# Spreading the relative-bias rows from SBUF in one transfer instead of by way of DRAM in two

## What is computed

```python
def run_trunk(x, ...):
    h = rmsnorm(x, g_attn)
    qa, ka, va, qb, kb, vb = split(h @ w_in)
    oa = window_sink_attention(qa, ka, va, sink_a, rel_bias)
    ob = axial_qknorm_attention(qb, kb, vb, gq_b, gk_b)
    x = x + concat(rmsnorm(oa), rmsnorm(ob)) @ w_out
    x = x + expert_choice_moe(rmsnorm(x, g_ffn), ...)
    x = x + sigmoid(rmsnorm(x, g_ple) @ w_ple_gate) * (p @ w_ple_proj)
    return rmsnorm(x, g_final)

# in window_sink_attention: 128 queries by 384 keys, 8 heads
rel = kj - WINDOW - qi
bias = rel_bias[t5_bucket(rel)]        # (128, 384) per head
s = q @ k * scale + bias
```

## Time and profile before

| | |
|---|---|
| Median of 3 runs | 1531.67 us (1531.56 to 1531.7) |
| The profiled execution | 1531.56 us; its span, first to last instruction, 1529.8 us |
| TensorE (PE) busy | 1422.8 us, 93% of the span |
| VectorE, ScalarE, GpSimd busy | 905.6, 728.1, 193.1 us |
| Mean granted TensorE clock | 0.964 |
| ACT's DMA queue, q10 | 1056 packets, 2.11 MB, 0.4% of 16 engines' span |
| Projection stage | about 0 to 243 us, TensorE busy 229.15 us of it |

### The profile page before, as it was taken

One profiled execution on the slowest core, in us unless ns is written; L12 is line 12 of the kernel. 1 busy time (PEld: TensorE's weight loads), 2 busy tenths in 40 slices (PEclk: granted clock), 3 DMA queues, 4 the chain that ended last, 5 costly groups with the idle time before them and its releaser, 6 DMA issues. The chain is left out here.

```text
span 1529.8 us, 21337 instructions
## 1 busy us (share of the span) xinstructions
PE 1422.8 (93%) x7224; PEld 1003.9 (66%) x7224; DVE 905.6 (59%) x1316; ACT 728.1 (48%) x1161; POOL 193.1 (13%) x257
## 2 busy tenths in 40 slices
PE   7999998999999788799999699999999999959997
PEld 5888886655555455588877456666666666638885
DVE  4644446777777588323377656766776676662433
ACT  5544446776667577322224444445444444433342
POOL 1211110000000000100001201211121122011220
PEclk9999998999999799899999799999999999989998
DMA  9444446122112324444334647787788778772331
GB/s 350 153 145 144 144 175 222 66 103 94 67 58 93 126 84 149 139 158 155 122 122 173 226 185 260 248 264 257 260 272 263 254 258 270 253 222 109 124 138 69
DMA packets 83750, 266.78 MB, mean 174 GB/s; under 512 B 8128, under 2 KB 37952, under 8 KB 68336
## 3 DMA queue, kind: packets, MB, share of 16 engines
q1 hardware_dynamic: 75472, 238.80, 43.4%
q0 software_dynamic: 7168, 25.17, 7.1%
q10 hardware_dynamic: 1056, 2.11, 0.4%
HBM read 201.55 MB, written 66.60 MB: 175 GB/s over the span
## 5 line engine op out<-in xcount | busy, mean ns | idle before, releaser
L1922 DVE TENSOR_TENSOR moe_w_lo<-ring,moe_w_hi 128x2048 fp32r<-128x2048 f32 x96 | 220.4, 2296 | 157.8 <-ACT moe_w_hi L1858 157.8
L1858 ACT ACTIVATE moe_w_hi<-ring 128x2048 fp32r<-128x2048 f32 x96 | 184.0, 1918 | 198.4 <-PE moe_p_g L2044 122.2
L1566 PE MATMUL mix_p_big<-kept_out_w,mix_m_hi 128*128 128x512 f32 x384 | 126.0, 410 | 4.9 <-DVE mix_m_lo L1441 2.7
L555 PE MATMUL proj_p_out<-proj_w_hi,proj_h_hi 128*128 128x512 f32 x288 | 118.2, 410 | 10.4 <-DVE proj_w_lo L465 10.2
L2052 PE MATMUL moe_p_gu<-ring,moe_xT_r 128*64 128x512 f32 x512 | 116.9, 598 | 0.0
L555 PE MATMUL proj_p_out<-proj_w_hi,proj_h_lo 128*128 128x512 f32 x288 | 113.7, 395 | 0.0
L555 PE MATMUL proj_p_out<-proj_w_lo,proj_h_hi 128*128 128x512 f32 x288 | 113.5, 394 | 0.0
L1090 DVE TENSOR_REDUCE sample_ntop<-sample_p_s 128x1 f32<-128x1024 f32 x64 | 78.2, 1222 | 37.1 <-PE sample_p_s L913 36.4
L927 PEld LDWEIGHTS sample_p_t<-kept_ident_r,sample_probs_r 128*128 128x128 f32 x688 | 72.8, 141 | 23.3 <-ACT sample_probs L1028 6.7
L1566 PEld LDWEIGHTS mix_p_big<-kept_out_w,mix_m_hi 128*128 128x128 f32 x384 | 72.5, 194 | 21.6 <-DVE mix_m_lo L1441 2.9
L927 PE MATMUL sample_p_t<-kept_ident_r,sample_probs_r 128*128 128x128 f32 x688 | 79.9, 245 | 5.0 <-ACT sample_probs L1028 2.6
(11 more groups left out here) (291 smaller groups left out, 3087.3 us busy)
## 6 DMA issues: line engine op xcount, KB each, us to landing
ring<-in_w_gate SPq DMA_DIRECT2D x32, 1024.0 KB, 5.2
ring<-in_w_up SPq DMA_DIRECT2D x32, 1024.0 KB, 7.1
ring<-in_w_down SPq DMA_DIRECT2D x32, 1024.0 KB, 6.8
qT_d<-proj_qT SPq DMA_DIRECT2D x12, 1024.0 KB, 3.8
proj_xT<-in_xT SPq DMA_DIRECT2D x12, 512.0 KB, 4.2
proj_w_raw<-in_w_in SPq DMA_DIRECT2D x8, 768.0 KB, 7.0
proj_x<-in_x SPq DMA_DIRECT2D x12, 512.0 KB, 4.7
kT_d<-proj_kT SPq DMA_DIRECT2D x12, 512.0 KB, 3.5
```

What stands on the lines that cost most here:

```text
L555: mm = pe.matmul(p_out[:, s, cols], h[:, s, k, :], w[:, k, cols], start=(k == 0 and n == 0), stop=(k == KC - 1 and n == 2))
L1566: mm = pe.matmul(p_out[:, cols], m[:, s, k, :], ww[:, k, cols], start=(k == 0 and n == 0), stop=(k == KC - 1 and n == 2))
L1858: act.activation(w_hi[:, at % SPLIT], raw[:, at % RAW], ACT.Copy).then_inc(hi_made, 1)
L1922: dve.tensor_tensor(w_lo[:, at % SPLIT], raw[:, at % RAW], w_hi[:, at % SPLIT].bitcast(F32), ALU.subtract).then_inc(lo_made, 1)
```

## The change

The first of the two transfers, its semaphore `out` and the scratch tensor `rel_rows_d` are removed. One transfer remains, issued on ACT where the first one was, in front of the two squares. Its source is now the SBUF tile `rows`, on 8 partitions, each row named 128 times; its destination is as before, but the heads are now the outermost dimension of the access pattern (8), the query positions the second (128), where before the query positions were outermost. It still sets `stored`.

```diff
-        self.landed, self.looked, self.added, self.out, self.stored = (
-            a.sem(n) for n in ("bias_landed", "bias_looked", "bias_added", "bias_out", "bias_stored"))
+        self.landed, self.looked, self.added, self.stored = (
+            a.sem(n) for n in ("bias_landed", "bias_looked", "bias_added", "bias_stored"))
...
-    def store(self, act, rows_d):
+    def store(self, act, rel_d):
+
         act.wait_ge(self.added, 1)
-        act.dma_start(rows_d, self.rows[:]).then_inc(self.out, 16)
-
-    def spread(self, act, rows_d, rel_d):
-
-        act.wait_ge(self.out, 16)
-        act.dma_start(bass.AP(rel_d.tensor, 0, [[HEADS * (REL + P) + 1, P], [REL + P, HEADS], [1, REL]]),
-                      bass.AP(rows_d.tensor, 0, [[0, P], [REL, HEADS], [1, REL]])).then_inc(self.stored, 16)
+        act.dma_start(bass.AP(rel_d.tensor, 0, [[REL + P, HEADS], [HEADS * (REL + P) + 1, P], [1, REL]]),
+                      self.rows[:].unsqueeze(1).broadcast_to([HEADS, P, REL])).then_inc(self.stored, 16)
...
-            bias.store(act, rel_rows_d)
+            bias.store(act, rel_d)
             square(0, 0)
             square(1, 1)
-            bias.spread(act, rel_rows_d, rel_d)
             post_middle(0, 0)
...
-    rel_rows_d, rel_d = scratch("rel_rows_d", (HEADS, REL)), scratch("rel_d", (P, HEADS, REL + P))
+    rel_d = scratch("rel_d", (P, HEADS, REL + P))
```

More of the change, by code:

```diff
@@ L161, in add, with project_inputs @@
         dve.tensor_tensor(self.rows[:], self.p_rows[:], self.outside[:], ALU.add).then_inc(self.added, 1)
-    def store(self, act, rows_d):
+    def store(self, act, rel_d):
         act.wait_ge(self.added, 1)
-        act.dma_start(rows_d, self.rows[:]).then_inc(self.out, 16)
-    def spread(self, act, rows_d, rel_d):
-        act.wait_ge(self.out, 16)
-        act.dma_start(bass.AP(rel_d.tensor, 0, [[HEADS * (REL + P) + 1, P], [REL + P, HEADS], [1, REL]]),
-                      bass.AP(rows_d.tensor, 0, [[0, P], [REL, HEADS], [1, REL]])).then_inc(self.stored, 16)
-def project_inputs(nc, kept, unit, x, xT, w_in, g_attn, gqk, rope, rel_bias, hot, outside, qT_d, kT_d, v_d, rel_rows_d, rel_d, ahead):
+        act.dma_start(bass.AP(rel_d.tensor, 0, [[REL + P, HEADS], [HEADS * (REL + P) + 1, P], [1, REL]]),
+                      self.rows[:].unsqueeze(1).broadcast_to([HEADS, P, REL])).then_inc(self.stored, 16)
+def project_inputs(nc, kept, unit, x, xT, w_in, g_attn, gqk, rope, rel_bias, hot, outside, qT_d, kT_d, v_d, rel_d, ahead):
     RING = 4
@@ L2316, in encoder_layer @@
         project_inputs(nc, kept, unit, i["x"], i["xT"], i["w_in"], i["g_attn"], i["gqk"], i["rope"], i["rel_bias"], i["hot"],
-                       i["outside"], qT_d, kT_d, v_d, rel_rows_d, rel_d, ahead)
+                       i["outside"], qT_d, kT_d, v_d, rel_d, ahead)
         mix_inputs = MixInputs(nc, kept, ahead.q_low, i["x"], mixed_d)
```

## The result

The changed kernel takes 1547.15 us as the median of 4 runs (1542.49 to 1547.25), the kernel before 1531.65. The ratio is 1.0094, with a 95% interval of 1.0075 to 1.0112. The forecast was no change, 1531.6 us and at most 1533.2; it was wrong. The profiled execution took 1540.53 us with a span of 1538.8, 9.0 more than before.

What follows compares the result with a forecast made beforehand. TensorE was taken to bound the projection stage, so ACT, POOL or DMA gains count nothing. The profiled execution's 1531.56 us plus four zero terms gave 1531.6 us, no change, range 1530.4 to 1533.2.

Steps and rivals of the forecast that it cites:

- What bounds the kernel: Projection stage: TensorE sets the pace, waiting 0.2 us in all from 25 to 200 us; gains elsewhere are worth nothing.
- removed wait: ACT, second transfer's issue (0.65 us) and the wait before it: lie in time ending with TensorE's product anyway; gain 0.
- moved issue: ACT, ahead of the two squares: 0.65 us issue makes squares 0.1 us later, within POOL's 4.77 us idle; costs 0.
- early landing: Bias data for the reader issued at 199.31 us: already 158 us early, so landing earlier gains 0.
- The transfer's price: ACT's DMA queue: 0.099 us a packet, 128 on each of eight engines, 12.7 us; no effect on the sum.
- What it collides with: SP's loads on shared DMA engines: all through at about 45.2 us, ahead of the q store at 51.61; costs 0.
- Rival A: Slow source partitions delay tile 0's k store behind the transfer; at 0.30 us a packet TensorE stands 4.4 us, 1536.0; chance 0.04.
- B: ACT's issue blocks until descriptors have room; held 10.0 us, 4.6 us reach TensorE, 1536.2; chance 0.03.
- C: Transfer cut into 512 B pieces, 4096 packets, 25 us an engine; still 1531.6, counted within no change's 0.89.
- D: Faster: only moved DRAM addresses could gain over 0.2 us, put at 1 us, 1530.6; faster by over 0.2%: 0.03.

Runs made afterwards that it cites:

- e1: Kernel before, both transfers kept, the second written heads outermost on both sides, source still DRAM; 1530.47 us, ratio 0.9995.
- e2: Changed kernel with the eight source rows on SBUF partitions 0, 4, ..., 28 in place of 0 to 7; 1530.24 us, ratio 0.9997.
- e10: Changed kernel with the eight source rows on SBUF partitions 0, 2, ..., 14 in place of 0 to 7; 1531.58 us, ratio 1.0004.
- e4: Changed kernel with its transfer cut into eight, one per head, query positions outermost, each reading one partition; 1581.58 us, ratio 1.0327.

## Why the prediction was wrong, step by step

**What bounds the kernel; removed wait, moved issue, early landing.** Right. ACT's idle time behind the issue is 7.25 us (before 7.95), the squares start at 25.76, the issue took 0.55. `ahead_bias` was issued late only because everything was; no run waited for `stored`.

**The transfer's price: the step that failed.** I took "128 x 0.099 = 12.7" us for each of eight engines, with 0.099 from a transfer whose source was DRAM. The eight engines were right; a packet takes 0.316 us, and 128 of them 40.4. I had nearly this as an estimate, 0.30, by the ports of the Trainium skill ("SBUF — State Buffer", "Door 1: The DMA port swizzle"), and still gave 0.04 to the rival that rests on it. The trace of before had no row on a source of few partitions, and I let the nearest row stand for it, though it differs in just the thing that the change alters. e1, e2 and e10 show that nothing else does it: 0.089 from DRAM, 0.091 from eight groups, 0.148 from four, 0.315 from two, and e4 1.10 from one, on twice the engines.

**What it collides with.** "All is through at about 45.2 us", and so ahead of the q store, follows from the price and fell with it: with 0.316 the same sum gives 25.2 + 7.3 + 40.4 = 72.9, and the transfer ran until about 73 us. The slacks I had read held for all loads (rope rows, xT and x of tiles 2 and 3 kept nobody waiting), though x of tiles 2 and 3 took 19.4 and 22.5 us to land where 5.0 was usual.

**Rival A** named the mechanism, and its price of 0.30 is near the measured one, but it named the wrong store. I had counted that engines serve the two queues in turn, packet by packet; then the q store with its 8 large packets an engine would be 2.4 us later and the k store with 64 would matter. In the rows SP's packets on the shared engines don't come in turn: none in 60 to 65 us, and the q store goes with the transfer's end, 18 us late, against the 6.0 us between its usual landing (51.61 + 4.0) and ACT's need at 61.65. Landing at 50.77 + 21.9 = 72.7, it is 11.8 us behind the need at 60.9. A's sum had 4.4; with the measured 0.316 it gives 37.7 + 40.4 = 78.1, 6.4 us late, and 1538.0 in place of the measured 1547.15. So the right price alone would not have given the time: the held q store was missing too. The lower clock after the wait, another 2.8, was in no sum.

**Rivals B, C, D.** B isn't seen in the changed kernel (issue 0.55); e4 shows that it exists with eight transfers in line. C isn't: rows of 2 KB, 1024 of them. D: none.

## What to carry to other kernels

A DMA source of a few neighbouring SBUF partitions that is read many times runs at the rate of those partitions, not of the engines: here 24 to 27 GB/s for each group of four. Price a new kind of source by itself, and where no row shows it, a wide gap to the nearest row is a reason to widen the range, not to take the row. A transfer with 158 us of slack for its own reader still kept TensorE waiting 11.5 to 12.5 us for another: ask of each store on the other queue that shares its engines whether it can wait until the slow transfer is over. Here spreading the rows two or four partitions apart, or keeping the pieces out of the stores' way, undid the loss; no version beats the kernel before, since TensorE never waited for the removed hop.

## What the runs showed of the hardware that was not expected

- Two queues on the same DMA engines did not share them evenly here, where one was slow at its source. In the changed kernel the loads of x came through in 42 to 50 us, but SP's packets stood still on the shared engines for stretches of over 5 us (none of SP's queue in 60 to 65). What decides whose turn it is was not tried.
- Eight transfers of 256 KB from one partition each held the issuing engine for 56.4 us in all (e4), while a single one of 2 MB was issued in 0.55 us. Whether their number or the slow source did it was not tried.
- The wait of 11.45 us cost TensorE 14.3: it was followed by about 5.6 us at half the clock (0.50 granted in 70 to 75 us).
